# Spreading a VectorE selection over the steps of an attention loop, and an earlier split of one weight chunk

## What is computed

```python
def conformer_conv(u_val, u_gate, conv_w, conv_b, ln_g, ln_b, w_pw2):
    a = u_val * sigmoid(u_gate)
    y = depthwise_causal_conv(a, conv_w) + conv_b        # 31 taps, 512 channels
    return silu(layernorm(y, ln_g, ln_b)) @ w_pw2

def block_fn(blk, q_b, qi_b, w_b):                        # 128 queries, 8 blocks
    s_raw = einsum("bthd,bsd->bths", qi_b, k_idx)
    score = einsum("bth,bths->bts", w_b, relu(s_raw))
    score = where(causal, score, -inf)
    _, sel = top_k(score, 256)                            # ties: the earliest keys
    logits = einsum("bthc,btkc->bthk", q_b, kv[sel]) * 128 ** -0.5 + bias
    probs = softmax(where(valid, logits, -inf))
    return einsum("bthk,btkc->bthc", probs, kv[sel])      # 8 heads
```

## Time and profile before

| | before |
|---|---|
| median of 3 | 3219.48 us |
| lowest to highest | 3214.33 to 3221.94 us |
| span of the profiled execution | 3213.2 us |
| TensorE, matmul busy | 3009.0 us, 94% |
| TensorE, weight load busy | 1864.1 us, 58% |
| VectorE busy | 1870.8 us, 58% |
| ScalarE busy | 1109.3 us, 35% |
| GpSimd busy | 1033.7 us, 32% |
| mean granted TensorE clock | 0.966 of full speed |

### The profile page before, as it was taken

One profiled execution on the slowest core, in us unless ns is written; L12 is line 12 of the kernel. 1 busy time (PEld: TensorE's weight loads), 2 busy tenths in 40 slices (PEclk: granted clock), 3 DMA queues, 4 the chain that ended last, 5 costly groups with the idle time before them and its releaser, 6 DMA issues.

```text
span 3213.2 us, 48564 instructions
## 1 busy us (share of the span) xinstructions
PE 3009.0 (94%) x19842; PEld 1864.1 (58%) x19842; DVE 1870.8 (58%) x3077; ACT 1109.3 (35%) x1972; POOL 1033.7 (32%) x1000
## 2 busy tenths in 40 slices
PE   7979987999979978989999999999999989999998
PEld 7439865884439657864555555555565434444443
DVE  2575796773589986644365365365365374545455
ACT  2353545662366635643222222232122221111112
POOL 2301365000512570002512412422322235555552
PEclk9988998999989989999999989999989999999999
DMA  7423232002201330022111101101102101111111
GB/s 243 138 59 106 82 120 86 15 22 99 89 14 43 120 129 28 14 83 77 66 40 40 53 27 40 53 27 40 53 27 92 41 27 53 53 53 53 53 53 73
DMA packets 49165, 207.13 MB, mean 64 GB/s; under 512 B 4488, under 2 KB 9776, under 8 KB 32304
## 3 DMA queue, kind: packets, MB, share of 16 engines
q1 hardware_dynamic: 42288, 195.63, 17.7%
q10 hardware_dynamic: 6656, 8.39, 0.8%
HBM read 187.22 MB, written 16.79 MB: 63 GB/s over the span
## 4 chain that ended last, share of the span: by engine, by line
PE 78%; DVE 16%; ACT 3%; issue 3%; POOL 1%; DMA 0%; SPq 0%; DVEq 0%; ACTq 0%; POOLq 0%
PE big L275 16%; PE big L276 16%; PE big L277 16%; PE banks L275 6%; PE banks L277 5%; PE banks L276 5%; PE banks L1052 4%; DVE arena L1771 2%; PE banks L911 2%; DVE arena L1996 1%; PE big L587 1%; PE banks L587 1%; DVE arena L2160 1%; DVE arena L1976 1%; PE banks L590 1%
## 5 line engine op out<-in xcount | busy, mean ns | idle before, releaser
L557 POOL TENSOR_TENSOR w_lo<-stage,w_hi 128x512 bf16<-128x512 f32 x464 | 594.7, 1315 | 398.2 <-ACT w_hi L1239 397.5
L550 POOL CAST w_hi<-stage 128x512 bf16<-128x512 f32 x376 | 248.6, 704 | 1427.3 <-PE big L277 1232.3
L275 PE MATMUL big<-ht_hi,w_hi 128*128 128x512 bf16 x1184 | 448.7, 379 | 11.7 <-DVE arena L2023 6.5
L277 PE MATMUL big<-ht_hi,w_lo 128*128 128x512 bf16 x1184 | 448.7, 379 | 0.0
L276 PE MATMUL big<-ht_lo,w_hi 128*128 128x512 bf16 x1184 | 448.7, 379 | 0.0
L275 PE MATMUL big<-w_hi,ht_hi 128*128 128x256 bf16 (+1 forms) x1280 | 384.6, 300 | 20.8 <-POOL w_lo L557 9.1
L276 PE MATMUL big<-w_lo,ht_hi 128*128 128x256 bf16 (+1 forms) x1280 | 384.1, 300 | 0.0
L277 PE MATMUL big<-w_hi,ht_lo 128*128 128x256 bf16 (+1 forms) x1280 | 383.4, 300 | 0.0
L1784 DVE TENSOR_SCALAR_CACHE_REDUCE arena<-arena,smalli 128x512 bf16<-128x512 f32 (+5 forms) x268 | 206.7, 827 | 2.4
L275 PEld LDWEIGHTS big<-ht_hi,w_hi 128*128 128x128 bf16 x1184 | 117.6, 99 | 147.9 <-issue 11.4
L277 PEld LDWEIGHTS big<-ht_hi,w_lo 128*128 128x128 bf16 x1184 | 115.8, 98 | 139.7
(11 more groups left out here) (361 smaller groups left out, 6666.8 us busy)
## 6 DMA issues: line engine op xcount, KB each, us to landing
stage<-in_w SPq DMA_DIRECT2D x130, 1024.0 KB, 4.8
arena<-in_w_ada SPq DMA_DIRECT2D x48, 512.0 KB, 4.3
arena<-in_x SPq DMA_DIRECT2D x16, 512.0 KB, 7.4
xs<-arena SPq DMA_DIRECT2D x16, 512.0 KB, 2.6
arena<-xs SPq DMA_DIRECT2D x16, 512.0 KB, 9.1
gt<-arena ACTq DMA_DIRECT2D x16, 256.0 KB, 2.5
arena<-gt ACTq DMA_DIRECT2D x16, 256.0 KB, 2.7
out_x<-arena SPq DMA_DIRECT2D x8, 512.0 KB, 2.6
```

The costliest lines, as they stand in the source:

```text
L275: pe.matmul(out, ah, bh, start=start, stop=False)
L277: return pe.matmul(out, al, bh, start=False, stop=stop)
L550: pool.tensor_copy(w_hi[:, n % RING, c0:c1], stage[:, n % RAW_RING, c0:c1]).then_inc(s_w_hi_split, mark(s_w_hi_split, n, q))
L557: ins = pool.tensor_tensor(w_lo[:, n % RING, c0:c1], stage[:, n % RAW_RING, c0:c1], w_hi[:, n % RING, c0:c1], ALU.subtract)
```

## The change

The choice leaves its place between the search and `split_normed`. Its five instructions become the parts 0 to 4 of a function `choose(tb, part)`; in attention, block tb's part is done during the steps of block tb-1: part 0 in step 2, part 1 (the scan) in step 3, and so on to part 4 in step 6. In a step it comes behind the queries' low part (L1969) and ahead of the output's scaling (L2015 to L2020). The two scratch rows move from PB, which attention uses, to a place of their own, CHOICE, which was the normalised convolution's. The layer-norm sums and the shift (`beside(34)`, `beside(35)`) now follow the search directly. In ScalarE's list conv_high(10) moves from behind the fourth gate tile of g2 to behind the second.

```diff
+        CHOICE = [fl(4096, 1024), fl(5120, 1024)]
...
                 for tp in range(4):
                     gate_by_token(0, tp)
-                conv_high(10)
+                    if tp == 1:
+                        conv_high(10)
                 gate_by_token(1, 0)
...
-                for j, tb in enumerate(TBS):
-                    N = (tb + 1) * P
-                    beside(32 + j)
+                beside(34)
+                beside(35)
+
+                def choose(tb, part):
+
+                    j, N = tb - TBS[0], (tb + 1) * P
                     thr = f_end[:, j:j + 1].bitcast(F32)
-                    eq, run = PB[0][:, 0:N], PB[1][:, 0:N]
-                    step(dve.tensor_scalar(eq, score[tb], thr, None, ALU.is_equal))
-                    step(dve.tensor_tensor_scan(run, eq, eq, 0.0, ALU.add, ALU.max))
-                    step(dve.scalar_tensor_tensor(eq, run, s_(S_KEEP + j), eq, ALU.is_le, ALU.mult))
-                    step(dve.scalar_tensor_tensor(eq, score[tb], thr, eq, ALU.is_gt, ALU.add))
-                    step(dve.tensor_scalar(score[tb], eq, -1.0, NEG, ALU.add, ALU.mult))
+                    eq, run = CHOICE[0][:, 0:N], CHOICE[1][:, 0:N]
+                    if part == 0:
+                        step(dve.tensor_scalar(eq, score[tb], thr, None, ALU.is_equal))
+                    elif part == 1:
+                        step(dve.tensor_tensor_scan(run, eq, eq, 0.0, ALU.add, ALU.max))
+                    elif part == 2:
+                        step(dve.scalar_tensor_tensor(eq, run, s_(S_KEEP + j), eq, ALU.is_le, ALU.mult))
+                    elif part == 3:
+                        step(dve.scalar_tensor_tensor(eq, score[tb], thr, eq, ALU.is_gt, ALU.add))
+                    else:
+                        step(dve.tensor_scalar(score[tb], eq, -1.0, NEG, ALU.add, ALU.mult))
+
                 for n in range(4):
                     split_normed(n)
...
                     if i < n and steps[i][1] == 3 and steps[i][0] < NT - 1:
                         queries(steps[i][0] + 1)
+                    if i < n and steps[i][0] + 1 in TBS and 2 <= steps[i][1] < 7:
+                        choose(steps[i][0] + 1, steps[i][1] - 2)
```

## The result

| | before | after |
|---|---|---|
| median of 4 | 3218.86 us | 3245.91 us |
| lowest to highest | 3214.33 to 3221.94 | 3242.83 to 3250.02 |
| ratio, 95% interval | | 1.0096 [1.0079, 1.0113] |
| span of the profiled execution | 3213.2 us | 3242.0 us (its time: 3243.81) |
| attention begins in layer 0, layer 1 | 540.61, 1219.54 | 534.92, 1227.77 |

Attention is counted from the first product of its queries to its last output transpose.

A forecast was written before the change was run, and what follows sets the result against it. TensorE, busy 94%, was taken as the bound, VectorE equally in attention's steps 3 to 5. Span 3213.2 - 24.2 + 38.0 = 3227.0; median 3219.48 plus 13.8 gave 3233.3 us, forecast's own range 3220 to 3243, 8-of-10 range 3211 to 3243.

The forecast's parts named there:

- The gain ahead of attention: Before attention: earlier second gate half, full clock and earlier L1834 save 11.5 and 12.7 us per layer, 24.2 in all.
- the normalisation keeps its distance from the gate tiles: Behind the second gate half: convolution sums ready at 471.1, before ScalarE wants them at about 471.7, so no delay.
- The prediction's own sign of being wrong: Forecast is wrong if attention grows under 12 us in a layer, or the stretch before it shrinks under 8.
- the scan of block 6: Attention, block 6: scan takes 3.17 us beside GpSimd's weight splitting; with parts 2 and 3 the block costs 4.74.
- The cost in attention: Thirty choice instructions per layer, queued on VectorE in blocks 1 to 6, cost 19.0 us per layer, 38.0 for both.
- The waits that were to show it: In attention, TensorE's waits before the output's turn L934 were to be 2 us and more in blocks 1 to 3.
- Hidden parts: Rival: VectorE, busy 58%, has room for the moved parts in attention, so only the gain shows; 3195.3 us, chance 0.10.
- only short blocks: Rival: in attention only blocks 1 to 3 pay, 16.1 us lost, blocks 4 to 6 catch up; 3211.4 us, chance 0.12.
- the first rival: The rival that the moved parts are hidden in attention, by VectorE's 58% occupancy; 3195.3 us, chance 0.10.
- Nothing absorbed: Rival: in attention parts 0, 2 and 4 count too, up to 69 us against 24.2; 3264 us, chance 0.08.
- The early copy that doesn't pay: Rival: raw chunk lands after 453.25, so cv10's 3 us wait stays in each layer; 3239.5 us, chance 0.08.
- The rule about shared reading: Two-SBUF-input VectorE instructions and SBUF-reading GpSimd ones block each other; applied to block 6's scan, 0.8 us per layer.

The follow-up runs named there:

- e1: The changed kernel with the layer norm's shift reading its second input from PSUM, one reciprocal added; 3229.78 us, ratio 1.0041.
- e5: The changed kernel, but GpSimd takes up weight chunk pw2 only when the shift is done; 3231.68 us, ratio 1.0043.
- i1: The changed kernel with an unused two-input tensor_tensor of 512 columns added ahead of the batch-norm sums in both layers; 3234.39 us, ratio 1.0060.
- e4: The changed kernel without the calls of choose, so the choice of keys isn't computed at all; 3206.19 us, ratio 0.9967.
- f2: e1 with the scan ahead of L1969, in blocks 1 to 3 part 2 too (block 1 also part 3), the rest in steps 6 and 7; 3193.11 us.
- h2: The changed kernel with an unused two-input tensor_tensor added: layer 0 ahead of the batch-norm sums, layer 1 between sums and aggregation; 3236.96 us.

## Why the prediction was wrong

- **The gain ahead of attention, 24.2 us: right in itself, then lost.** The steps up to the gate tiles came out as worked: after tile 1's activation the second half starts 8.5 us earlier in layer 0 and 8.6 us in layer 1 (8.6 forecast), at full clock, and `split_normed` waits for ScalarE. Where the shift isn't held, the stretches ahead of attention are shorter than in before by 27.2 us (e1), 24.6 (e5) and 24.3 (i1), both layers together. e1, which takes the held shift away and nothing else, gives 3229.78 us, 12.3 above before; 38.0 - 24.2 = 13.8 had been forecast.
- **The step that failed** is the sentence that the convolution's sums are ready before ScalarE wants them, "so the normalisation keeps its distance from the gate tiles". The sums were ready, at 469.12, 23.2 us after tile 1's activation (23.1 forecast). But the "so" passes over the next link, the shift, which stands at nothing in the sum. It took 11.65 us instead of the 0.20 of before, since the change takes away the choices that ran beside GpSimd's row ahead of it; i1 shows that one such instruction, early in the row, is enough to spare it. This cost 16.6 us by the rows of ScalarE, and 16 to 19 us by the stretches ahead of attention, 8.2 us shorter in after and 24.3 to 27.2 in the three runs named. The prediction's own sign of being wrong, a stretch ahead of attention that shrinks by less than 8 us, is there: 3.6 and 4.5. It priced the shared reading of VectorE and GpSimd in one place only, the scan of block 6.
- **The cost in attention, 19.0 per layer: right in mechanism and size,** 18.2. The distances from one L935 to the next (the first from the beginning of attention) grew in blocks 1 to 6 by 2.46, 2.80, 2.83, 3.00, 3.21 and 3.83 us, where 2.32, 2.85, 2.86, 2.86, 3.38 and 4.74 were forecast. The waits that were to show it are there: L935 in layer 0, block 2, of TensorE in after, with the earlier trace rows for before (1.33 us in block 1, 1.04 in block 3):

```profile
585.61 0.66 PE L935 MATMUL big<-con,arena 128*128 128x128 f32 x4 [1.19 <-DVE arena L2033]
```

  They are about half of the 2 us and more that I named: the rest of the delay is met in the steps before. Block 6 was mis-sized, 3.83 for 4.74: I took 3.17 us for the scan at 1024 columns beside GpSimd; it took 2.32 (L1962, mean of the two), since it came up in a cast's last 0.18 us and went ahead of GpSimd's subtraction.
- **The rivals.** Hidden parts (3195.3) are ruled out by e4: without the choices attention is shorter by 37.8 us, and the time by 39.7; only short blocks (3211.4) by the growth of blocks 4 to 6, 10.0 of 18.1 us. The Trainium skill (Perfetto Trace Analysis, Identifying the Most-Contended Engine) takes the engine of highest occupancy as the one to improve; it gives no price for work put on another one, and the first rival's reading of it as such doesn't hold here: VectorE is at 58% in before, after and f2, and the same work cost 18 us or at most 1.4 us per layer by its place in the queue. Nothing absorbed (3264) would have needed 34 us per layer, 18 were measured. The early copy that doesn't pay (3239.5) is ruled out by the wait of 0.24 us; that it is the nearest in number to the median is chance, since its mechanism isn't there.
- **The rule about shared reading.** The rows first: VectorE instructions that came up early in GpSimd's row lost at most 1.06 us, the shift 11.5. By the Trainium skill (SBUF — State Buffer, Who interferes with whom) the side that comes second is blocked until the first one's instruction is over; most of the early ones agree with that, and those that came up in an instruction's last 0.1 us waited for the next one as well. By this rule the shift, which came up 0.11 us into a cast of 0.62, would have taken some 0.7 us, and the kernel some 16 us less. Here the measurement differs from the rule, and it decides.

## What to carry to other kernels

When work is moved off an engine, price again what stays there: it may have been fast only because of what ran beside it, here a VectorE instruction of 0.2 us that took 11.65 once no other VectorE work came between GpSimd's instructions. Where a long row of GpSimd instructions runs beside VectorE, give VectorE a two-input instruction in it early, take one of its operands from PSUM, or let GpSimd pause. And place inserted work ahead of the instruction that ends the engine's idle time, not behind it: the same thirty instructions cost 18 us or at most 1.4 us per layer.

## What the runs showed of the hardware

- VectorE is shut out by an unbroken row of GpSimd instructions once this is long: with 12 or fewer done it lost 1.06 us at most (some 3000 instructions of the kind counted above, in the 17 traces), with 13 or more (10.63 us) it was held to the row's end in all 16 cases, for up to 16.69 us. All 16 lie at this one place of the kernel, with the batch-norm instructions near. h2 (layer 0) and i1, where the shift comes behind all of these and takes 0.43 and 0.45 us, show that they alone aren't the cause. (In nine traces a tensor_scalar of 1024 columns in the next block, L2057 in before, also came up behind 15 instructions of a row, but in the row's last one, so it tells nothing.) An instruction with one SBUF input and 512 columns was held as well (14.56 us); the 128x8 reciprocal (0.20 us), the batch-norm sums (0.68) and the shift with one input in PSUM (0.16) weren't. Why a long row shuts VectorE out stays open.
- GpSimd pays too when VectorE gets its turn: beside the added instruction of h2 its cast took 1.08 us instead of 0.61, and beside the scan of after (2.32 us, at 688.72) its subtraction took 3.13 us instead of 1.16.
- The stall also costs clock: TensorE's granted clock, at full in the twenty microseconds before in all three runs, was 0.83 in 469 to 489 us of after and 0.84 in 489 to 509. In the same two windows it was 0.91 and 1.00 in e1, and 1.00 and 0.83 in i1.
